# A hybrid SSD, gMLP and conv-FFN block on one core: split weights of the mixer kept in DRAM, and all weight sums made in one mixer

## The reference

```python
h = rmsnorm(x, norm1_g) * (1 + sc1) + sh1
x = x + g1 * hybrid_mixer(h, ...)      # one projection to 4624 columns, conv, SSD scan, spatial gating, one out projection
h = rmsnorm(x, norm2_g) * (1 + sc2) + sh2
x = x + g2 * conv_gated_ffn(h, ...)    # up to 2 x 2816, causal conv of width 3, silu gate, down
return rmsnorm(x, final_g)

def conv_gated_ffn(h, w_up, conv_w, conv_b, w_down):
    gate, val = jnp.split(h @ w_up, 2, axis=-1)
    gate = causal_dwconv(gate, conv_w, conv_b)
    return (jax.nn.silu(gate) * val) @ w_down
```

## Time and profile before

| what | us |
|---|---|
| median of 3 runs | 3005.82 (2995.24 to 3006.25) |
| the profiled execution | 3002.1 |
| its span | 3000.4 |
| PE busy | 2748.2 (92%) |
| DVE busy | 2013.8 (67%) |
| POOL busy | 1557.0 (52%) |
| ACT busy | 1157.5 (39%) |
| DMA | 447.78 MB, mean 149 GB/s |

### The profile page before, as it was taken

One profiled execution on the slowest core, in us unless ns is written; L12 is line 12 of the kernel. 1 busy time (PEld: TensorE's weight loads), 2 busy tenths in 40 slices (PEclk: granted clock), 3 DMA queues, 4 the chain that ended last, 5 costly groups with the idle time before them and its releaser, 6 DMA issues.

```text
span 3000.4 us, 34711 instructions
## 1 busy us (share of the span) xinstructions
PE 2748.2 (92%) x12391; PEld 2219.8 (74%) x12391; DVE 2013.8 (67%) x2612; ACT 1157.5 (39%) x1786; POOL 1557.0 (52%) x1056
## 2 busy tenths in 40 slices
PE   1889999899999999989977999999999999998994
PEld 1567878677877888877765788877887788887773
DVE  4677885778567655558666778667765845555868
ACT  0354334533343333343424533364334433334332
POOL 0666644676446777544564434444344544444455
PEclk9999999999999999999989999999999999999997
DMA  8454543645445655563333333343234333446333
GB/s 317 151 180 161 175 166 116 197 162 193 144 150 169 214 189 198 172 239 111 117 109 109 106 103 107 121 152 108 85 120 138 123 123 122 125 127 243 91 114 121
DMA packets 234376, 447.78 MB, mean 149 GB/s; under 512 B 22773, under 2 KB 80601, under 8 KB 229595
## 3 DMA queue, kind: packets, MB, share of 16 engines
q1 hardware_dynamic: 230450, 442.60, 44.8%
q10 hardware_dynamic: 3754, 2.96, 0.3%
HBM read 366.69 MB, written 78.78 MB: 148 GB/s over the span
## 4 chain that ended last, share of the span: by engine, by line
PE 65%; DVE 14%; issue 9%; POOL 5%; DMA 4%; ACTq 1%; ACT 1%; SPq 0%; DVEq 0%; POOLq 0%
PE main L1648 25%; PE main L1895 12%; PE pair L1895 12%; PE main L1909 4%; PE pair L1909 4%; POOL w_lo L571 3%; PE pair L1770 2%; DVE a_lo L1340 1%; DMA w_raw<-in_ff_down_dram 1%; DVE acc L1126 1%; DVE stats L985 1%; POOL tb L582 1%; PE pair L1755 1%; PE pair L1795 1%; PE pair L1762 1%
## 5 line engine op out<-in xcount | busy, mean ns | idle before, releaser
L571 POOL TENSOR_TENSOR w_lo<-w_raw,w_hi 128x512 fp32r<-128x512 f32 x880 | 1274.5, 1454 | 1338.6 <-ACT w_hi L679 1330.1
L679 ACT ACTIVATE w_hi<-w_raw 128x512 fp32r<-128x512 f32 x880 | 549.3, 629 | 1497.6 <-PE main L1648 577.6
L1648 PE MATMUL main<-w_hi,h_hi 128*128 128x512 f32 x768 | 321.6, 419 | 0.6 <-POOL w_lo L571 0.6
L1648 PE MATMUL main<-w_hi,h_lo 128*128 128x512 f32 x768 | 301.5, 393 | 0.0
L1648 PE MATMUL main<-w_lo,h_hi 128*128 128x512 f32 x768 | 301.1, 392 | 0.0
L1340 DVE TENSOR_TENSOR a_lo<-g,a_hi 128x512 fp32r<-128x512 f32 x132 | 181.1, 1379 | 132.7 <-ACT a_hi L898 132.3
L1403 DVE SCALAR_TENSOR_TENSOR c_acc<-c_gate,col_b,c_acc 128x512 f32<-128x512 f32 x176 | 208.1, 1222 | 3.7 <-ACT c_acc L865 1.4
L582 POOL TENSOR_TENSOR tb<-tb,tb 128x512 f32<-128x512 f32 x132 | 201.3, 1525 | 0.0
L1648 PE MATMUL main<-h_hi,w_hi 128*128 128x512 f32 x384 | 155.7, 405 | 40.3 <-POOL w_lo L571 25.7
L1648 PEld LDWEIGHTS main<-w_hi,h_hi 128*128 128x128 f32 x768 | 146.4, 191 | 38.0 <-issue 8.5
L1648 PEld LDWEIGHTS main<-w_lo,h_hi 128*128 128x128 f32 x768 | 145.9, 190 | 36.5 <-issue 8.4
(11 more groups left out here) (288 smaller groups left out, 6212.9 us busy)
## 6 DMA issues: line engine op xcount, KB each, us to landing
w_raw<-in_w_in_dram SPq DMA_DIRECT2D x288, 256.0 KB, 2.9
w_raw<-t_up_scratch SPq DMA_DIRECT2D x176, 256.0 KB, 2.7
w_raw<-in_ff_up_dram SPq DMA_DIRECT2D x132, 256.0 KB, 3.0
w_raw<-in_w_out_dram SPq DMA_DIRECT2D x128, 256.0 KB, 2.8
ada_t<-in_ada_w_dram SPq DMA_DIRECT2D x24, 1024.0 KB, 13.8
w_raw<-t_down_scratch SPq DMA_DIRECT2D x90, 256.0 KB, 2.6
tb<-in_ff_up_dram SPq DMA_DIRECT2D x88, 256.0 KB, 4.1
t_up_scratch<-tb SPq DMA_DIRECT2D x88, 256.0 KB, 2.9
```

What stands on the lines that cost most here:

```text
L571: nc.gpsimd.tensor_tensor(w_lo[:, g % RING, :], w_raw[:, g % RING, :], w_hi[:, g % RING, :].bitcast(F32), ALU.subtract).then_inc(w_lo_ok, 1)
L679: nc.scalar.activation(w_hi[:, g % RING, :], w_raw[:, g % RING, :], ACT.Copy).then_inc(w_hi_ok, 1)
L1648: ins = T.matmul(main[i], a, w, start=first and p == 0, stop=last and p == 2)
```

## The change

Mixer 0 splits its weights as before, into one array `w_hl` that holds both parts of a slot side by side, and SP stores each slot's two parts (512 KB) into DRAM (`hl_d`). Mixers 1 to 3 load the two parts straight into `w_hl` and split nothing; such a load waits until PE has used unit n-4. No sums are made in mixer 0 and in FFN 0; all 33 are made in mixer 1, every two units from unit 16, and stored four units after their load. In mixers 1 to 3 POOL and ACT have no weights to split.

Beside that: large transfers (x2, h2, y, x, g) are issued as smaller ones beside successive units; block 0's output is stored beside units 18 to 25, the tiles of `half1_scale` first; the finish of DVE for block 1 becomes `finish1` and for s = 0 stands in mixer 2 between `dt_biased` and the dt chain; `bc_tok` takes all of B and C'B in one ACT copy, the mask is applied to it in SBUF, and PE no longer waits for the mask before the product with the state; `xn2_last` comes after `seed(0)`; the last two products of the up half go to sets 2 and 3.

```diff
-    UP_SET = [2, 0, 1, 0, 1] + [(2, 3, 0, 1)[n % 4] for n in range(NUP - 5)]
+    UP_SET = [2, 0, 1, 0, 1] + [(2, 3, 0, 1)[n % 4] for n in range(NUP - 7)] + [2, 3]
-        w_hi, _ = fixed("w_hi", [P, RING, W], F32R)
-        w_lo, _ = fixed("w_lo", [P, RING, W], F32R)
+        w_hl, _ = fixed("w_hl", [P, RING, 2, W], F32R)
+        w_hi, w_lo = w_hl[:, :, 0, :], w_hl[:, :, 1, :]
+        hl_d = nc.dram_tensor("w_split_scratch", [MU, P, 2, W], F32, kind="Internal").ap()
-        T_OF = (range(0, 11), range(11, 21), range(21, 33))
-        T_AT = ([4 + 7 * i for i in range(11)], [16 + 13 * i // 2 for i in range(10)], [18 + 10 * i for i in range(12)])
+        T_OF = (range(0), range(0, 33), range(33, 33))
+        T_AT = ((), [16 + 2 * i for i in range(33)], ())
         def t_set(t):
-            return t % 2 if t < T_OF[2][0] else 1
+            return t % 2
...
+            def store_split(n):
+                sp.wait_ge(w_lo_ok, n + 1 + RING)
+                sp.dma_start(hl_d[n], w_hl[:, n % RING, :, :].bitcast(F32)).then_inc(hl_st[n % RING], 16)
+
+            def load_mixer(b, n, src):
+                if b == 0:
+                    load(n, src)
+                    if n >= RING:
+                        store_split(n - RING)
+                else:
+                    if b == 1 and n < RING:
+                        store_split(MU - RING + n)
+                        sp.wait_ge(hl_st[n], 16 * (MU // RING))
+                    if b == 2 and n < RING:
+                        sp.wait_ge(w_lo_ok, split_no(mix0(b) - RING + n) + 1 + RING)
+                    sp.wait_ge(w_used, mix0(b) + n + 1)
+                    sp.dma_start(w_hl[:, n % RING, :, :].bitcast(F32), hl_d[n]).then_inc(hl_in[n % RING], 16)
...
-                if b == 2 and n == 23:
-                    store_y(0, 0)
-                    store_y(0, 1)
+                if b == 2 and 18 <= n < 18 + NT:
+                    store_y(0, 1, n - 18)
+                if b == 2 and 22 <= n < 22 + NT:
+                    store_y(0, 0, n - 22)
                 if b < 2:
                     for t, at in zip(T_OF[b], T_AT[b]):
-                        if n == at + 10:
+                        if n == at + 4:
                             t_store(t)
                         if n == at:
                             t_load(t)
...
             def low(g):
+                if RING <= g < MU:
+                    pool.wait_ge(hl_st[g % RING], 16 * (g // RING))
-            for b in range(2):
-                for n in range(MU):
-                    low(mix0(b) + n)
-                    for t, at in zip(T_OF[b], T_AT[b]):
-                        for step in range(4):
-                            if n == at + (0, 1, 3, 5)[step]:
-                                t_step(t, step)
+            for n in range(MU):
+                low(n)
+            for t in T_OF[1]:
+                for step in range(4):
+                    t_step(t, step)
...
             def split(g):
-                if g >= UNITS:
+                if g >= UNITS or loaded(g):
                     return
...
-                    if n == 0:
-                        xn2_last(b)
                     if n == 1:
                         seed(0)
+                        xn2_last(b)
...
+                if b == 2:
+                    finish1(0)
                 dve.wait_ge(dt_soft, b + 1)
...
+            def weights_in(b, n):
+                if b:
+                    pe.wait_ge(hl_in[n % RING], hl_full(b, n))
+                else:
+                    pe.wait_ge(w_lo_ok, n + 1 + RING)
...
-                    pe.wait_ge(cbm_ok, b * NT + (cc + 1))
```

More of the change, by code:

```diff
@@ L314, in hybrid_decoder_trunk, with loaded, split_no, hl_full @@
         H_LO_AT = [P5 * KG + o for o in (8, 9, 9, 10, 12, 12, 13, 14)]
+        hl_in, hl_st = [sem(f"hl_in{n}") for n in range(RING)], [sem(f"hl_st{n}") for n in range(RING)]
+        g2y_in, fg_in = sem("g2y_in"), sem("fg_in")
+        def loaded(g):
+            return any(mix0(b) <= g < mix0(b) + MU for b in range(1, NB))
+        def split_no(g):
+            return g - MU * len([b for b in range(1, NB) if g >= mix0(b) + MU])
         def slot_full(g):
-            return 16 * (g // RING + 1)
+            return 16 * (split_no(g) // RING + 1)
+        def hl_full(b, n):
+            return 16 * ((b - 1) * (MU // RING) + n // RING + 1)
         block = ctx.enter_context(nc.Block())
@@ L391, in store_x2 @@
                 sp.wait_ge(xn_act_ok, 2 * b + 2)
[L392 to L397, removed]
-            def beside(b, n):
[L400 to L404, removed]
-                if b == 2 and n == 23:
-                    store_y(0, 0)
-                    store_y(0, 1)
+                sp.dma_start(x2_d[b, t], x2[:, t, :]).then_inc(x2_st, 16)
@@ L425, in beside @@
+                if n == OUT + 17 + NT:
                     sp.wait_ge(gate_stored, 16)
                     sp.dma_start(g_bc[:], gate_d[0:1, :].broadcast_to([P, D])).then_inc(x2_in, 16)
[L427 to L430, removed]
+                if b % 2 == 0 and OUT + 7 <= n < OUT + 7 + NT:
+                    t = n - OUT - 7
+                    if t == 0:
+                        sp.wait_ge(gm_tr, b * KD + KD)
+                    sp.dma_start(xnew[:, t, :], xv[b + 1, t]).then_inc(x_in, 16)
@@ L439, in mixer @@
                         beside(b, n)
-                        load(mix0(b) + n, rows(w_in, k)[:, COL_U + cc * W:COL_U + (cc + 1) * W])
+                        load_mixer(b, n, rows(w_in, k)[:, COL_U + cc * W:COL_U + (cc + 1) * W])
                         if k == 5:
@@ L453, in mixer @@
                         beside(b, Z + j * KD + k)
-                        load(mix0(b) + Z + j * KD + k, rows(w_in, k)[:, j * W:(j + 1) * W])
+                        load_mixer(b, Z + j * KD + k, rows(w_in, k)[:, j * W:(j + 1) * W])
                 for j in range(2):
@@ L544, in _ @@
                     ffn(b // 2)
-            store_y(NSB - 1, 1)
-            store_y(NSB - 1, 0)
+            for t in range(NT):
+                store_y(NSB - 1, 1, t)
+            for t in range(NT):
+                store_y(NSB - 1, 0, t)
             sp.wait_ge(y_stored, 16 * 2 * NT * NSB)
-            sp.wait_ge(w_lo_ok, UNITS + RING)
+            sp.wait_ge(w_lo_ok, split_no(UNITS) + RING)
         @block.gpsimd
@@ L632, in _ @@
                     final_gain(s)
-                if b < NB:
-                    for n in range(MU):
-                        low(mix0(b) + n)
-                        if b == 2 and n == 8:
-                            final_gain(0)
+                if b == 2:
+                    final_gain(0)
         @block.scalar
@@ L1524, in down, with finish1 @@
                         half_stats(1, 0, 2 * (k - 8) + 1)
+                if s == NSB - 1:
+                    finish1(s)
+            def finish1(s):
                 dve.wait_ge(pool_fin, s * 6 + 6)
@@ L1639, in _, with unit @@
                          ).then_inc(gate_mm, 1)
-            def unit(n_at, G_at, first, last, mms):
-                pe.wait_ge(w_lo_ok, n_at)
+            def weights_in(b, n):
+                if b:
+                    pe.wait_ge(hl_in[n % RING], hl_full(b, n))
+                else:
+                    pe.wait_ge(w_lo_ok, n + 1 + RING)
+            def unit(b, n, G_at, first, last, mms):
+                weights_in(b, n)
                 for i in range(4):
@@ L1761, in chunk_state @@
                     for g in range(2):
-                        last = T.matmul(aux[g], b_tok[:, g, :], xdec[:, g * W:(g + 1) * W], start=True, stop=True)
+                        last = T.matmul(aux[g], bc_tok[:, g, :], xdec[:, g * W:(g + 1) * W], start=True, stop=True)
                     last.then_inc(s_done, 1)
```

184 lines of the change are left out of this document (103 added, 81 removed).

## The result

The changed kernel takes 3075.19 us (median of 4), the kernel before 3004.55; the ratio is 1.0243, 95% interval 1.022 to 1.0265. The forecast was slower, 3051 us with a range of 3010 to 3096.

What follows compares the result with a forecast made beforehand. TensorE was taken as busiest in every stage, with DMA to bound the sums in mixer 1. Terms: +104 there, -20 mixer 0, smaller gains elsewhere, +11 at da_t, summing to +49 on 3002: 3051 us, range 3010 to 3096.

Steps and rivals of the forecast that it cites:

- The period of the sums: Units 16 to 81 of mixer 1: DMA bytes plus a pause make 33 periods of 10.8 us, +104 us.
- The low end of my own case: Sums in mixer 1 with a pause of 1.5 us and a period of 10.2, counted under "same".
- the band of no change: Whole kernel: totals of 2991 to 3021 us, within 0.5%, count as the same; chance 0.10.
- Mixer 0 without sums: Mixer 0 loses eleven sums, hides its stores of split weights and falls towards mixer 3: -20 us.
- Up and down halves: Up half 0 without sums -4, first down products -9, seed(0) -7, smaller pieces of g -5; the seam -7.
- The 2.76 us on a burst of g: Wait before the last up products, behind large transfers of g; smaller pieces were to give -5 us for two.
- two single terms: First down products find banks free (wait of 4.56 us), -9; seed(0) ahead of xn2_last (wait of 3.92 us), -7.
- The seam and mixer 2: Start of mixer 2 -7 us, transpose of da_t +11, wait on late weights -1, two smaller POOL waits -4.
- `bc_tok`: All mixers: PE no longer waits 2.82 us for DVE's mask before the first y_off product; -9 us, mixer 1 hiding it.
- The queue stays full: Rival, mixer 1: no pause, period 8.8 us, stretch +38, total 2985 us; chance 0.10.
- The clock falls: Rival, mixer 1: PE at the lower 1.2 GHz clock throughout, work 14.3 us per period, total 3167 us; chance 0.10.
- Starving mixers 2 and 3: Rival: SP's waits delay loads with a lead of only four units, +24 us, total 3075; chance 0.12.

Runs made afterwards that it cites:

- the first three experiments: Changed kernel with the sums spread as before the change: 2926.68 us; each sum stored one unit earlier: 3014.55; 30 of 33 sums moving a quarter of their rows: 2945.61.
- fourth experiment: Changed kernel with three quarters of each split weight's columns not loaded in mixer 1, number and order of DMAs unchanged: 2984.52 us.
- The fifth and sixth experiment: Changed kernel with finish1(0) moved ahead of the wait for the transposed dt: 3067.82 us; with block 0's output stored beside units 25 to 29: 3063.21 us.

## Why the prediction was right, point by point

**The period of the sums: mechanism right, two sizes too small.** `t_load` waits for the landing of a store issued on the same unit, the queue runs dry, and DMA sets the pace: the timeline, the share of 0.10 and the first three experiments show each part. The size: 10.8 us were predicted for a period, 413.2 / 33 = 12.5 came. At a share of 0.78 that is 9.8 us of work and 2.7 dry; predicted were 8.8 and 2.0. The bytes were right: 262 GB/s x 413.2 us = 108 MB, 3.28 MB per period. The rate was not. I priced the split weights at the 417 GB/s of the prologue's loads; they ran at some 325 (fourth experiment), and the whole mixture at 262 / 0.78 = 336, where the earlier trace rows had 356. In sum +160.5 us in the stretch where +104 was predicted.

The row behind the 417 was misread: what moves there is not rows of 4 KB only. Most of its bytes are 1 MB tiles of `ada_w`, whose runs in DRAM are 8 KB long: the 372 packets of SP's queue in those 10 us carry 2.76 MB, 7.4 KB each. Nor does it take the mixture to bring the rate down: mixer 3 of the changed kernel, which moves split weights and no sums, runs at 199 / 0.60 = 332. Why these loads run below 417 stays open.

The dry time, too, came another way than I had it. I expected `t_load` some 3 us after the last store's issue; it comes 6.2 after (733.4 against 727.2). A store of a sum lands 7.1 us after its issue in the median here, where the same store took 2.9 in the kernel before, and most of SP's wait passes while the queue still works. The low end of my own case was also off: a pause of 1.5 gives a period of 10.3 and a total of some 3034, which is not in the band of no change.

The Trainium skill (DMA: Bandwidth & Descriptors, "Latency and other measured facts") puts a DMA's fixed cost at some 2 us and its larger part on HBM's latency, with up to 2 us for the latter under load. The 2.7 us dry per period lie above the first figure, in a queue that is loaded; the trace does not separate the two.

**Mixer 0 without sums: -23.4 (predicted -20).** The stores of the splits are hidden, as predicted, when no sums are there.

**Up and down halves: -55.6 in all (predicted -32 with the 7 of the seam).** The 2.76 us on a burst of g are gone, and the first down product starts with no wait for its bank. But two single terms were too large. Two units later PE waits 2.88 us for `a_lo` of DVE: I did not ask what is ready next. The transposes of the up half wait 2.98 us, now for `xn2_last`, of 3.92: that step moved the wait to the next in line. Against that the down halves gained 12 and 11 us (the first beside its 7 at the seam) that no term of mine had. PE's busy time fell there by 6.0 and 4.4 us, with the granted clock up from 0.94 to 0.99 and from 0.91 to 0.94, and its waits on `a_lo` by 6.9 and 6.2. The block of 2 MB of x_half became four transfers between weight loads; an idle time of 6.30 us of PE near 1473 in the trace before, on `a_lo`, has no match of that size after. That this edit did it is a guess from the trace, not tested.

**The seam and mixer 2: right in each part.** Start of the mixer 6.98 us idle (predicted 6.9), da_t 10.09 (12.2), the wait on late weights 13.06 (15.3 to 17.7). The fifth and sixth experiment take the last two away one at a time. All three waits are where the prediction put them. The one on da_t is shorter because the finish took 8.1 us on DVE, not 11.2; its first step took 2.29 us, with POOL idle, not 3.34 as in the earlier trace rows.

```profile
1689.37 2.29 DVE L1594 TENSOR_TENSOR x_half<-x_half,y_half 128x2048 f32<-128x2048 f32 x1
```

**`bc_tok`: mixer 3 -6.4 (some 3 predicted).** The 2.82 us before the product with the state are gone, and so are smaller waits on ACT and DVE (1.3 and 1.1) that no term had; it is 341.9 us at 341.5 busy.

**The rivals.** *The queue stays full* is false: the period was above 9.3 us even with the store a unit earlier (its mixer 1 is 108 us above the one before). *The clock falls*: it did, to 0.83 of full over the stretch, PE's busy time growing from 236.5 to 285.4; but that is 8.6 us in a period of 12.5, with 123.1 us of PE's waits for weights in the stretch and 3.3 of SP's for PE, so the queue still set the pace. The Trainium skill (TensorE: Matmul & The Clock Gate, "HAM oscillation") describes the low clock after DMA waits and counts it as time lost; the trace agrees that it comes, but shows room for it here, since the work still fits into the period. *Starving mixers 2 and 3* is false: mixer 3 has no idle time to speak of on four units of lead. That this rival's 3075 is the measured total is chance.

**The total.** The profiled span grew by 75.0 us where +49 was predicted; the miss of 26 us is 57 more in the stretch of sums and 6 ahead of mixer 0 and in the rest of mixer 1, less some 37 in the halves and in mixers 2 and 3. So 3051 stands close to 3075 in part by luck: two misses of opposite sign.

## What to carry to other kernels
Before moving transfers to where an engine is free, add up the bytes per period there, and price them at the rate of a row in which the same transfers move, not at the best rate in the trace. Look in the issuing queue's written order for a store whose landing is awaited by the very next load: one other transfer between them gave 61 us back here without moving a byte less. When a change combines a large idea with many small edits, undo them apart: here the small edits were worth some 62 us, the idea 17, and one placement cost 149.

## What the runs showed of the hardware
Loads that were mostly of 8 KB rows ran at 417 GB/s; the 4 KB rows of the split weights ran at some 325 beside sum loads and stores (fourth experiment), and mixer 3, which moves mostly them, at 332. A 256 KB store of a sum of up weights landed 7.1 us after its issue in the median, where it took 2.9 with the sums spread as in the kernel before. DVE's addition of [128, 2048] took 3.34 us while POOL worked and 2.29 while it did not; the five others of the later trace took 3.37 to 4.49.
